# Second attention of a two-block model: values by column halves, probabilities scaled before they are turned

## The reference

```python
def second_block(x, ...):
    u = rms_norm(h, mix_norm_g)
    q, k, v, glu_a, glu_g = jnp.split(u @ w_in, splits, axis=-1)   # 512 columns each
    attn_out = moba_attention(heads(q), heads(k), heads(v), rel_bias)   # 8 heads of 64
    conv_out = conformer_conv(glu_a, glu_g, conv_w, conv_b, conv_ln_g, conv_ln_b)
    h = h + jnp.concatenate([attn_out, conv_out], axis=-1) @ w_out
    u = rms_norm(h, ffn_norm_g)
    h = h + (jax.nn.silu(u @ w_gate) * (u @ w_up)) @ w_down
    return rms_norm(h, final_norm_g)

def conformer_conv(a, g, w_dw, b_dw, ln_g, ln_b):
    u = a * jax.nn.sigmoid(g)
    u = causal depthwise convolution of width 31 (u, w_dw) + b_dw
    mu, var over the 512 channels of a token
    return jax.nn.silu((u - mu) * lax.rsqrt(var + LN_EPS) * ln_g + ln_b)
```

## Time and profile before

| what | us |
|---|---|
| median of 3 runs | 1715.2 |
| lowest, highest | 1714.01, 1721.3 |
| the profiled execution | 1716.44 |
| its span, first to last instruction | 1714.2 |
| busy in it: PE, DVE, ACT, POOL | 1597.2, 923.5, 644.7, 142.2 |

### The profile page before, as it was taken

The page is one execution under the profiler, slowest core; times in us unless marked ns, Lnnn a source line. Parts: engine busy times, 40 slices in busy tenths (PEclk is TensorE's granted clock), DMA queues, the critical chain, the costliest instruction groups (busy, mean ns, idle before and its releaser), DMA issues. The chain is left out here.

```text
span 1714.2 us, 20713 instructions
## 1 busy us (share of the span) xinstructions
PE 1597.2 (93%) x7902; PEld 1324.8 (77%) x7902; DVE 923.5 (54%) x1377; ACT 644.7 (38%) x912; POOL 142.2 (8%) x108
## 2 busy tenths in 40 slices
PE   7997998999899979999999979689989999999997
PEld 5776986967788857888888858477778788888886
DVE  5745346368444456777752254677764444444223
ACT  5442431146332334444432133455354444443221
POOL 0003400000000010000000000268110000000000
PEclk9988999899899999999999989899989999999998
DMA  5210004100122312322223313222011222222231
GB/s 197 74 62 1 1 1 190 37 19 2 37 92 92 123 50 76 120 97 93 91 73 102 99 59 110 75 75 98 25 46 54 98 98 97 92 92 79 86 101 66
DMA packets 22688, 132.08 MB, mean 77 GB/s; under 512 B 2512, under 2 KB 2896, under 8 KB 12768
## 3 DMA queue, kind: packets, MB, share of 16 engines
q1 hardware_dynamic: 20960, 123.48, 20.6%
q0 software_dynamic: 800, 6.36, 1.0%
q10 hardware_dynamic: 864, 1.36, 0.2%
HBM read 129.09 MB, written 2.10 MB: 77 GB/s over the span
## 5 line engine op out<-in xcount | busy, mean ns | idle before, releaser
L306 PE MATMUL ps<-AH,whi 128*128 128x512 f32 x1280 | 511.5, 400 | 63.1 <-DVE AL L388 23.2
L307 PE MATMUL ps<-AL,whi 128*128 128x512 f32 x1280 | 505.6, 395 | 0.0
L308 PE MATMUL ps<-AH,wlo 128*128 128x512 f32 x1280 | 505.0, 395 | 0.0
L293 DVE TENSOR_TENSOR wlo<-raw,whi 128x2048 fp32r<-128x2048 f32 (+4 forms) x126 | 252.8, 2006 | 275.4 <-ACT whi L286 275.0
L306 PEld LDWEIGHTS ps<-AH,whi 128*128 128x128 f32 x1280 | 244.6, 191 | 127.4 <-issue 27.5
L308 PEld LDWEIGHTS ps<-AH,wlo 128*128 128x128 f32 x1280 | 244.7, 191 | 52.0
L307 PEld LDWEIGHTS ps<-AL,whi 128*128 128x128 f32 x1280 | 244.9, 191 | 49.5
L286 ACT ACTIVATE whi<-raw 128x2048 fp32r<-128x2048 f32 (+4 forms) x126 | 210.6, 1671 | 164.3 <-PE ps L308 164.3
L306 PE MATMUL ps<-HH,whi 128*128 128x512 f32 x352 | 136.9, 389 | 0.0
L307 PE MATMUL ps<-HL,whi 128*128 128x512 f32 x352 | 136.9, 389 | 0.0
L308 PE MATMUL ps<-HH,wlo 128*128 128x512 f32 x352 | 136.9, 389 | 0.0
(11 more groups left out here) (346 smaller groups left out, 2034.2 us busy)
## 6 DMA issues: line engine op xcount, KB each, us to landing
raw<-wstream SPq DMA_DIRECT2D x74, 1024.0 KB, 4.7
raw<-wstream SPq DMA_DIRECT2D x32, 704.0 KB, 3.9
raw<-wstream SPq DMA_DIRECT2D x16, 768.0 KB, 4.1
raw<-wstream SPq DMA_DIRECT2D x8, 640.0 KB, 3.7
hT<-xT SPq DMA_DIRECT2D x4, 512.0 KB, 7.9
W1k<-w1k_d POOLq DMA_DIRECT2D x1, 2048.0 KB, 10.2
W1v<-w1v_d POOLq DMA_DIRECT2D x1, 2048.0 KB, 15.7
raw<-wstream SPq DMA_DIRECT2D x2, 512.0 KB, 3.3
```

Of the source, the lines that this page charges most:

```text
L293: nc.vector.tensor_tensor(WL[b][:, 0:n], RAW[b][:, 0:n], WH[b][:, 0:n].bitcast(F32), ALU.subtract).then_inc(w_lo_done, 1)
L306: nc.tensor.matmul(out_, WH[b][:, w], xh[:, k, :], start=start and k == 0, stop=False)
L307: nc.tensor.matmul(out_, WH[b][:, w], xl[:, k, :], start=False, stop=False)
L308: last = nc.tensor.matmul(out_, WL[b][:, w], xh[:, k, :], start=False, stop=stop and k == n - 1)
```

## The change

- *Pairs.* The unit is now a pair of heads, 16 of them (`PAIRS2`), and the loop has 17 turns i = 2 to 18 on every engine (`ITER2`): in turn i `scores(i)`, `turn(i - 2)`, `values(i - 3)` on PE.
- *First scores.* `scores(0)` (banks 6 and 7) is issued between the two halves of V's projection, `scores(1)` (banks 2 and 3) before its last token tile. Their `top`s stand on DVE between the reads of V's banks.
- *Scaling.* DVE takes the reciprocal of the sums right after the exponentials (`factors`), and GpSimd multiplies the probabilities with it in place, before they are turned (`p2_scaled`). The product into `Y2` and `Y2` itself are gone.
- *Values.* 64 columns of `V2` are the weights and 128 queries of `PT2` move; the result is feature-major, one head of the pair on PSUM partitions 0 to 63, the other on 64 to 127, in bank 6. The transposes of `Y2` are gone; bank 6 holds a whole query tile (four pairs) and is saved into `AH` (`save_hi`) and `AL` (`save_lo`) in turns 7, 11, 15 and after the last.
- *Saves of `PT2`.* ACT saves both heads of pairs 0 to 7; from pair 8 DVE saves the first head (`DVE_SAVES`).
- *Convolution.* The 15 taps on DVE come three per turn. Mean, variance and rows move to bank 7 and to turns 7, 12 and 14; centring is divided over two pairs on GpSimd; the next two weight pieces are split in turns 8 and 10 (ACT), 9 and 11 (DVE); the product with the rows is in turns 15 and 16.
- *Output projection.* Its first two outputs take the chunks in the order 4, 5, 0, 1, 2, 3, 6, 7.

```diff
+            PR2 = sb("PR2", [P, 3, 2, S], F32, x)
+            PT2 = sb("PT2", [P, 2, 2, S], F32, x)
...
+        PAIRS2 = [(qt, h) for qt in reversed(range(T)) for h in range(0, NH, 2)]
+        PER_QT2 = len(PAIRS2) // T
+        ITER2 = range(2, len(PAIRS2) + 3)
+        DVE_SAVES = 8
...
+        TAPS_EACH, I_MEAN, I_SQUARE, I_VAR, I_STAGE, I_ROWS = 3, 7, 10, 12, 8, 14
...
+            return ps[:, 7 if c == 3 else 3 + c, :]
+
+        def s2_bank(p, b):
+
+            return 6 + b if p == 0 else 2 * (p % 2) + b
...
+            def turn(p):
+                qt, h = PAIRS2[p]
+                if p == 0:
+                    pe.wait_ge(tap_done, WHOLE)
+                for b in range(2):
+                    pe.wait_ge(p2_scaled, 2 * p + b + 1)
+                    if p:
+                        pe.wait_ge(pt2_sb[b], p)
+                    for kt in range(qt + 1):
+                        last = turned(ps[:, 4 + b, kt * P:(kt + 1) * P], PR2[:, p % 3, b, kt * P:(kt + 1) * P], ident[:, :])
+                    last.then_inc(pt2_ps, 1)
+
+            def values(p):
+                qt, h = PAIRS2[p]
+                q, first, final = p // PER_QT2, p % PER_QT2 == 0, p % PER_QT2 == PER_QT2 - 1
+                for b in range(2):
+                    pe.wait_ge(pt2_sb[b], p + 1)
+                if first:
+                    pe.wait_ge(y2_lo, q) if q else bank_read(pe, "v2", 3)
+                for kt in range(qt + 1):
+                    for b in range(2):
+                        last = nc.tensor.matmul(ps[side(b), 6, h // 2 * P:(h // 2 + 1) * P],
+                                                V2[:, kt, (h + b) * DK:(h + b + 1) * DK],
+                                                PT2[:, p % 2, b, kt * P:(kt + 1) * P],
+                                                start=first and kt == 0, stop=final and kt == qt)
+                last.then_inc(o3_ps, 1)
...
                 weights_ready(pe, "v2", 0, b)
+                if b:
+                    scores(0)
                 for t in range(T):
                     tok = slice(t * P, (t + 1) * P)
                     if b == 0:
                         bank_ready(pe, "v2", t)
+                    if b and t == 3:
+                        scores(1)
...
+            for i in ITER2:
+                if i < len(PAIRS2):
+                    scores(i)
+                if i - 2 < len(PAIRS2):
+                    turn(i - 2)
+                if i >= 3:
+                    values(i - 3)
...
-            pe.wait_ge(o3_done, n // 2)
-            for qt in range(T):
-                for c in range(4):
-                    last = turned(ps[:, y2_bank(qt), c * P:(c + 1) * P], Y2[:, qt, c * P:(c + 1) * P], ident[:, :])
-                last.then_inc(y2_ps, 1)
-            pe.wait_ge(y2_lo, T)
             weights_ready(pe, "wo2", 0, 0)
-            for k in range(DC):
-                if k >= 4:
-                    pe.wait_ge(cu_lo, k - 3)
+            for n, k in enumerate((4, 5, 0, 1, 2, 3, 6, 7)):
+                pe.wait_ge(cu_lo, k - 3) if k >= 4 else pe.wait_ge(y2_lo, T)
...
+            def probabilities(p):
+                n = (PAIRS2[p][0] + 1) * P
+                for b in range(2):
+                    act.wait_ge(s2_max, 2 * p + b + 1)
+                    if p >= 3:
+                        act.wait_ge(pt2_ps, 2 * (p - 3) + b + 1)
+                    nc.scalar.activation(PR2[:, p % 3, b, 0:n], ps[:, s2_bank(p, b), 0:n], ACT.Exp, bias=NM2[:, 2 * (p % 2) + b, :],
+                                         accum_out=LS2[:, p % 4, b:b + 1]).then_inc(p2_ready, 1)
+
+            def save_hi(q):
+                qt = T - 1 - q
+                act.wait_ge(o3_ps, PER_QT2 * (q + 1))
+                nc.scalar.activation(AH[:, 0:4, qt * P:(qt + 1) * P], ps[:, 6, :].rearrange("p (c n) -> p c n", c=4),
+                                     ACT.Copy).then_inc(y2_hi, 1)
...
+            def factors(p):
+                dve.wait_ge(p2_ready, 2 * p + 2)
+                if p >= 4:
+                    dve.wait_ge(p2_scaled, 2 * (p - 4) + 2)
+                vec.reciprocal(RL2[:, p % 4, :], LS2[:, p % 4, :]).then_inc(rl2_ready, 1)
+
+            def save_lo(q):
+                qt = T - 1 - q
+                tok = slice(qt * P, (qt + 1) * P)
+                dve.wait_ge(y2_hi, q + 1)
+                vec.tensor_tensor(AL[:, 0:4, tok], ps[:, 6, :].rearrange("p (c n) -> p c n", c=4),
+                                  AH[:, 0:4, tok].bitcast(F32), ALU.subtract).then_inc(y2_lo, 1)
+
+            taps(len(left) - (CT - SPLIT))
             top(0)
+            save_v(0)
+            save_v(1)
             top(1)
-            for u in range(n + 1):
-                if u + 2 < n:
-                    top(u + 2)
-                if u and u % 2 == 0:
-                    add(u // 2 - 1)
-                if u == 0:
-                    bank_read(dve, "v2", 3)
-                taps(1)
-                if u == U_MEAN + 1:
+            factors(0)
+            save_v(2)
+            save_v(3)
+            for i in ITER2:
+                if i - 1 < len(PAIRS2):
+                    factors(i - 1)
+                if i < len(PAIRS2):
+                    top(i)
+                if i >= PER_QT2 + 3 and i % PER_QT2 == 3 and i < ITER2[-1]:
+                    save_lo(i // PER_QT2 - 1)
+                if DVE_SAVES <= i - 2 < len(PAIRS2):
+                    save_pairs(dve, vec.tensor_copy, i - 2, 0)
+                taps(TAPS_EACH)
...
+            for p in range(len(PAIRS2)):
+                n = (PAIRS2[p][0] + 1) * P
+                pool.wait_ge(rl2_ready, p + 1)
+                for b in range(2):
+                    x = PR2[:, p % 3, b, 0:n]
+                    nc.gpsimd.tensor_scalar(x, x, RL2[:, p % 4, b:b + 1], None, ALU.mult).then_inc(p2_scaled, 1)
+                if I_MEAN + 1 <= p < I_MEAN + 3:
+                    pool.wait_ge(mu_ready, 1)
+                    for c in (2 * (p - I_MEAN) - 2, 2 * (p - I_MEAN) - 1):
+                        nc.gpsimd.tensor_tensor(CU[:, c, :], CU[:, c, :], TMP[:, 0, :], ALU.subtract).then_inc(centred, 1)
```

More of the change, by code:

```diff
@@ L1603, in norm_mean @@
                 for c in range(CC):
-                    last = nc.tensor.matmul(ps[:, 3, :], ones[:, :], CU[:, c, :], start=c == 0, stop=c == CC - 1)
+                    last = nc.tensor.matmul(ps[:, 7, :], ones[:, :], CU[:, c, :], start=c == 0, stop=c == CC - 1)
                 last.then_inc(mu_ps, 1)
@@ L1611, in norm_var @@
                     for t in range(T):
-                        last = nc.tensor.matmul(ps[:, 3, t:t + 1], UG[:, c, t * P:(t + 1) * P], ones[:, 0:1],
+                        last = nc.tensor.matmul(ps[:, 7, t:t + 1], UG[:, c, t * P:(t + 1) * P], ones[:, 0:1],
                                                 start=c == 0 and t == 0, stop=c == CC - 1 and t == T - 1)
                 last.then_inc(var_ps, 1)
-            n = len(UNITS2)
-            scores(0)
-            scores(1)
-            pe.wait_ge(tap_done, WHOLE)
@@ L1620, in blk2_pe @@
-            for u in range(n + 1):
-                if u % 2 == 0 and u + 2 < n:
-                    scores(u + 2)
-                    scores(u + 3)
-                if u < n:
-                    turn(u)
-                if u:
-                    values(u - 1)
-                if u == U_MEAN:
+            for i in ITER2:
[5 more added lines that the diff above has]
+                    values(i - 3)
+                if i == I_MEAN:
@@ L1648, in blk2_pe @@
                 for m in range(2):
[L1649 to L1651 removed]
+                    ins = product(y_bank(m), 0, 8 * m + k, 1, AH[:, k:k + 1, :], AL[:, k:k + 1, :], start=n == 0,
+                                  stop=n == DC - 1)
+                    if n == DC - 1:
                         ins.then_inc(seg_done, 1)
@@ new lines, in save_hi @@
+            def save_hi(q):
[3 more added lines that the diff above has]
+                                     ACT.Copy).then_inc(y2_hi, 1)
+            probabilities(0)
+            probabilities(1)
+            act.wait_ge(last_tap_done, len(LATE_TAPS))
+            for i in ITER2:
+                if i >= PER_QT2 + 3 and i % PER_QT2 == 3:
+                    save_hi(i // PER_QT2 - 1) if i < ITER2[-1] else None
+                if i < len(PAIRS2):
+                    probabilities(i)
+                for b in range(2):
+                    if i - 2 < len(PAIRS2) and (b or i - 2 < DVE_SAVES):
+                        save_pairs(act, nc.scalar.copy, i - 2, b)
+                if I_SQUARE <= i < I_SQUARE + 2:
+                    for c in (2 * (i - I_SQUARE), 2 * (i - I_SQUARE) + 1):
+                        act.wait_ge(centred, c + 1)
+                        nc.scalar.activation(UG[:, c, 0:S], CU[:, c, :], ACT.Square).then_inc(csq_ready, 1)
+                if i in (I_STAGE, I_STAGE + 2):
+                    stage_hi(act, "v2", 0, (i - I_STAGE) // 2, True)
+                if i == I_VAR + 1:
@@ L1717, in blk2_act @@
```

(11 more changed lines are left out.)

157 lines of the change are left out of this document (52 added, 105 removed).

## The result

The changed kernel took 1725.94 us (median of 8 runs, 1724.47 to 1730.02) against 1714.61: a ratio of 1.0069, 95% interval 1.005 to 1.0087. Timed again later beside three variants it was 1725.5 us, 1.0046 (1.0028 to 1.0064). So it is slower by 8 to 11 us; 1714 was forecast, at most 1722. All ratios and medians here leave out four executions, three of the variant with the mean first and one of the kernel before, that took 2323 to 3128 us.

What follows compares the result with a forecast made beforehand. DVE was taken to decide while taps are left, PE afterwards. Product 2.9 us earlier, plus 1.5 for the clock, gave -1.4: 1716.4 to 1715.0 profiled, median 1.2 lower, 1713.8, say 1714; range 1705 to 1722.

Steps and rivals of the forecast that it cites:

- The middle: Turns 7 to 11: 14.3 us of DVE and 3.2 us of waits; variance ends at 1268.5, six turns follow to 1281.2.
- The mean waits for the taps: Start of the middle turns: the mean waits for the taps and runs from 1245.3 to 1248.8.
- some 10 us earlier: Two splits of the next weights, 1.9 us on ACT and 2.3 on DVE, come that much earlier in the stage.
- the turn with taps: Turns 2 to 6, three taps each: DVE takes 4.29 us at 512 keys and 4.05 at 384.
- the column halves: Values on PE: 2.1 us per pair if halves follow one another, 1.05 plus 0.2 if they overlap; no effect taken.
- rival (c): Values' weight loads not hidden, 33.9 us instead of 19.6, so PE decides from turn 3: 1719.5 us; chance 0.06.
- the gap of 4.4 us ahead of the product: PE idle after values(15) through save, table load, Silu, copy and DVE's difference, before the second output projection: 4.4 us.
- scaling: GpSimd's multiplication per head at 512 columns: 1.3 us upper value, 0.7 lower; hidden while taps last.
- Rival (b): GpSimd is the bound at turn(i-2): over 0.5% slower from 2.3 us per scaling, 1727 at 2.6; chance 0.05.
- Clock: Lower PE clock after the gap before the output product: 1.5 us charged, between 0 and 2.9; nothing in the loop.
- Rival (d): Clock drops inside the loop because PE waits more: 11 us over five turns, 1725; chance 0.06.
- First scores inside V's projection: Two pairs' scores within V's projection: two pairs done early, 2.9 us lost, top(2) starting at 1224.3.

Runs made afterwards that it cites:

- the covered splits: Changed kernel with scores one turn ahead, attention chunks first, and weight splits ahead of the saves in turns 8 and 13: 0.9986 of the kernel before.
- the three edits: Changed kernel with weight splits behind the variance, scores one turn ahead and output chunks in order 0 to 7: 1718.6 us, 1.0018 of the kernel before.
- the last version: Changed kernel with scores ahead, attention first, splits ahead of the saves, and the mean's products ahead of values(4): 0.9984 of the kernel before.

## Why the prediction was wrong

- **The failed step is "The middle", its sentence "The mean waits for the taps".** I had save_lo in DVE's sum (2 x 0.7 us) but not as something that PE waits for. One bank holds a whole query tile, values(4) and values(8) wait for its copies, and mean, next scores and variance queue behind. By the count from V the prediction has the mean at 47.9, its end at 51.4, the variance at 66.4 to 71.1 and the product at 89.2. Measured: 52.5, 57.4, 76.5 to 83.5, 101.9. The 12.7 us are 4.6 for the mean's start, 1.4 for its length, 4.1 between mean and variance, 2.3 for the variance's length, 0.3 behind it. Of the 4.6 us, 0.7 are taps that ended late; the other 3.9 are the wait and values(4), for the mean put first starts at 48.6, when the last tap ends. That edit shows the cause: product 5.6 us earlier at an equally slow variance (1.2 of them the mean's own length), 0.0023 of the time. The second wait was not priced alone.
- **Between mean and variance** I summed DVE's work and added 3.2 us of waits; I counted one split there and gave the move "some 10 us earlier" no effect of its own. Before, ACT's part of the first ran under the variance and DVE's parts behind it; now they are on DVE's and ACT's path. Shown by the covered splits, 0.0032 against the three edits without cover. Delaying them alone did not help. The scores ahead alone gave 1.0032; with attention first and cover besides, 0.9986.
- **Right:** the turn with taps (4.44 and 4.16 us from top to top, against 4.29 and 4.05), the end of the last tap (48.6 against 47.4), and the column halves, 16 records in 1.03 us from start to start, less than the 1.25 of my lower end, without effect. "TensorE: Matmul & The Clock Gate", Part 3, in the Trainium skill says in its list of what overlaps that weights load during running products only where the row group differs; 0.064 us per record at 128 moving columns, while a load's record alone is 0.133 to 0.137 us long, shows these two halves overlapped, loads too, so the trace does not bear that out here, and it decides against the rival (c). (Its "19.6" us for the hidden case follows from no row; 160 records at 0.131 would be 21.0.) Right too was the gap of 4.4 us ahead of the product (4.29) with 2.7 us of it due to the chunks' order.
- **Mis-sized:** scaling, 1.56 us at 512 columns against my upper value of 1.3, that is 0.29 + 0.0025 per column. It is hidden in the turns with taps. "GPSIMD Engine Reference", section 3.1, of the Trainium skill led to an estimate of 0.77; the row is twice that. Rival (b) needed 2.3. With the splits covered the scaling costs up to 4.6 us.
- **Clock.** I charged 1.5 us at the product; from its first record to the span's end it is 424.7 us before, 426.7 after (426.4 to 427.1 in the variants), so 2.0. The size was near, the reason was not the gap of 4.4 us. In the variants with attention first the gap is 1.50 us and the loss the same (426.5 to 427.1 us). Behind the variance the grant was 0.50 for most of the time already. In the loop I charged nothing but a variance of 4.7 us. The mean and the variance at half clock cost 1.2 and up to 3 us (7.0 us in one execution, 4.2 in another of the same kernel). Rival (d) had the right sign and the wrong place: it is not the turns with taps, 1.00 throughout, but the turns with waits behind them.
- **"First scores inside V's projection"** was to move the taps, and the mean starts 3.5 us earlier than before (52.5 against 56.0). Put back, this part costs 2.3 us of product start at equally short variances: it is worth something, and the waits behind it cost more.

Open: why full or half clock falls on the variance in executions of one kernel, what the second wait for save_lo costs by itself, and what cover would give without the scores ahead. Single edits differ by hardly more than the timings can tell; the 0.6% between the changed kernel and the last version stands clear of them.

## What to carry to other kernels

When an accumulator goes from two buffers to one, look up who waits for its reader, and what is queued behind that waiter: here two waits of 3 us held the products that all four engines needed. Where a long product stops every engine, put independent work of the other engines right ahead of the instruction in which they wait, and issue the next round's inputs ahead of the product; here the inputs ahead alone gave 1.0032 against 1.0046, which is not told apart, and both, with attention first, 0.9986. Price a wait by an edit on the waiting engine's own order, not by moving work on engines that are part of the chain.

## What the hardware showed beyond that

- Two DVE scalings of 128x256, SBUF to SBUF with a factor per partition, took 0.62 us alone and 1.62 and 2.73 us beside GpSimd's two-input subtraction, which took 2.70 and 2.54 us for two, little over its 2.50. "SBUF — State Buffer", section "Who interferes with whom", in the Trainium skill has the two engines exclude each other on a shared pair of ports for a whole instruction when VectorE is in a two-port mode, which this operation can enter; DVE waiting out a GpSimd instruction of 1.27 us agrees with these rows.
- GpSimd's two subtractions that met a DVE split of weights took 4.54 us, and the split 2.91 instead of 2.28.
- From 1272 to 1304 PE was granted 0.50 and was busy for 81% of it; in the tap turns, 1224 to 1248, it was granted 1.00 throughout and was busy for 67%.
- Products of two column halves (64 columns of weights, 128 moving) took 0.064 us a record when the halves alternated and 0.094 when one half followed the other.
